# Ten modulation steps of the first FFN: from TensorE row products to weighted sums on VectorE

## What is computed

```python
c_act = silu(c)                                        # 1024 numbers
for l in range(2):
    shift1, scale1, gate1, shift2, scale2, gate2 = split(c_act @ ada_w[l] + ada_b[l], 6)
    if l == 1:
        k_shift, k_scale = split(c_act @ kv_ada_w + kv_ada_b, 2)
    ...
    h = modulate(rms_norm(x, norm2_g[l]), shift2, scale2)
    x = x + gate2 * ((silu(h @ w_gate[l]) * (h @ w_up[l])) @ w_down[l])
```

## Time and profile before

| | |
|---|---|
| median of 3 runs | 1451.62 us (1445.99 to 1454.34) |
| profiled execution: time, span | 1443.54 us, 1441.7 us |
| TensorE busy | 1355.0 us (94%) |
| VectorE busy | 794.1 us (55%) |
| ScalarE busy | 623.7 us (43%) |
| GpSimd busy | 86.3 us (6%) |
| granted TensorE clock, mean | 0.959 |

### The profile page before, as it was taken

One profiled execution on the slowest core, in us unless ns is written; L12 is line 12 of the kernel. 1 busy time (PEld: TensorE's weight loads), 2 busy tenths in 40 slices (PEclk: granted clock), 3 DMA queues, 4 the chain that ended last, 5 costly groups with the idle time before them and its releaser, 6 DMA issues.

```text
span 1441.7 us, 27270 instructions
## 1 busy us (share of the span) xinstructions
PE 1355.0 (94%) x11892; PEld 1241.3 (86%) x11892; DVE 794.1 (55%) x1040; ACT 623.7 (43%) x810; POOL 86.3 (6%) x79
## 2 busy tenths in 40 slices
PE   5579789999999989999999999999999999999998
PEld 4467689999996445999999999999998888999997
DVE  5964664343443365656655565644635755766543
ACT  4742354343343544554434544434542443644342
POOL 6522300000000011000000000000000000000000
PEclk8669799999999989999999999999998999999999
DMA  9606468996564247255556555456353434455452
GB/s 254 197 3 221 134 191 288 306 284 219 179 202 161 88 146 234 88 161 190 175 156 189 184 174 173 160 162 203 95 170 118 146 118 148 143 178 183 159 179 93
DMA packets 237798, 246.91 MB, mean 171 GB/s; under 512 B 5544, under 2 KB 233336, under 8 KB 237704
## 3 DMA queue, kind: packets, MB, share of 16 engines
q1 hardware_dynamic: 236968, 243.82, 53.2%
q0 software_dynamic: 480, 1.57, 0.6%
q10 hardware_dynamic: 256, 0.14, 0.0%
HBM read 244.47 MB, written 1.05 MB: 170 GB/s over the span
## 4 chain that ended last, share of the span: by engine, by line
PE 86%; DVE 6%; ACT 4%; DMA 2%; issue 1%; POOL 0%; SPq 0%; DVEq 0%; ACTq 0%
PE PS L1616 85%; DMA RING<-in_ada_w 1%; DVE ARENA L1397 1%; ACT PARTS L602 0%; DMA RING<-in_w_kv_b 0%; PE PS L2163 0%; DMA RING<-in_w_in 0%; DVE ARENA L1225 0%; DVE ARENA L1222 0%; DVE ARENA L1228 0%; DVE ARENA L1265 0%; DVE WL L1030 0%; DVE ARENA L1411 0%; DVE ARENA L1227 0%; DVE ARENA L1226 0%
## 5 line engine op out<-in xcount | busy, mean ns | idle before, releaser
L1616 PE MATMUL PS<-PARTS 128*128 128x256 f32 (+3 forms) x3652 | 850.4, 284 | 0.0
L1616 PEld LDWEIGHTS PS<-PARTS 128*128 128x128 f32 (+1 forms) x3652 | 627.6, 190 | 1.8 <-issue 1.0
L1030 DVE TENSOR_TENSOR WL<-RING,PARTS 128x2048 fp32r<-128x2048 f32 (+2 forms) x189 | 387.5, 2054 | 295.5 <-ACT PARTS L602 294.9
L1616 PE MATMUL PS<-HH,WL 128*128 128x256 f32 (+3 forms) x1832 | 526.2, 287 | 8.8 <-DVE PARTS L1301 4.0
L1616 PE MATMUL PS<-HH,PARTS 128*128 128x256 f32 (+3 forms) x1832 | 523.0, 286 | 0.0
L602 ACT CAST PARTS<-RING 128x2048 fp32r<-128x2048 f32 (+2 forms) x189 | 323.7, 1715 | 303.5 <-DMA RING<-in_w_ffn_out 68.2
L1616 PEld LDWEIGHTS PS<-HH,WL 128*128 128x128 f32 (+1 forms) x1832 | 349.5, 191 | 15.0 <-issue 7.7
L1616 PEld LDWEIGHTS PS<-HH,PARTS 128*128 128x128 f32 (+1 forms) x1832 | 349.0, 191 | 0.4
L1616 PE MATMUL PS<-PARTS,WL 128*128 128x256 f32 (+1 forms) x832 | 236.0, 284 | 0.4 <-DVE PARTS L1517 0.4
L1616 PEld LDWEIGHTS PS<-PARTS,WL 128*128 128x128 f32 x832 | 157.7, 190 | 1.8 <-issue 1.2
L1616 PE MATMUL PS<-ARENA 128*32 128x63 f32 (+5 forms) x720 | 59.5, 269 | 3.1 <-issue 2.6
(11 more groups left out here) (294 smaller groups left out, 1096.4 us busy)
## 6 DMA issues: line engine op xcount, KB each, us to landing
RING<-in_w_ffn_in SPq DMA_DIRECT2D x44, 1024.0 KB, 5.1
RING<-in_ada_w SPq DMA_DIRECT2D x36, 1024.0 KB, 6.9
RING<-in_ffn_w_gate SPq DMA_DIRECT2D x22, 1024.0 KB, 5.4
RING<-in_ffn_w_up SPq DMA_DIRECT2D x22, 1024.0 KB, 5.4
RING<-in_w_in SPq DMA_DIRECT2D x20, 1024.0 KB, 5.2
ARENA<-in_ada_w SPq DMA_DIRECT2D x12, 1024.0 KB, 8.5
RING<-in_ffn_w_down SPq DMA_DIRECT2D x16, 768.0 KB, 4.4
RING<-in_w_ffn_out SPq DMA_DIRECT2D x16, 768.0 KB, 4.4
```

Source lines behind the costliest of these rows:

```text
L1030: V.tensor_tensor(WL[:, u % SLOTS, 0:w], RING[:, u % SLOTS, 0:w], WH[:, u % SLOTS, 0:w].bitcast(fp32), SUB)\
L1616: return nc.tensor.matmul(o, lhsT, rhs, start=start, stop=stop)
```

## The change

The rows on TensorE, the row copies and MODR are gone for the ten steps. A step becomes two half steps: 1 MB of ADW each (four of the eight k tiles, all 512 columns), which VectorE multiplies by `c_act` and sums into ROWS with four chained instructions (`ada_sum`). Half step n is done by VectorE in pair n for n = 0 to 10, ahead of its wait for silu; halves 11 to 16 stand between the `w_low` of the down projection, two to a chunk; 17, 18 and 19 stand ahead of VectorE's wait for the last chunk. TensorE keeps `ada_cols` (with a column of ones): steps 0 to 4 between the gate and the up unit of pairs 2, 4, 6, 8, 10; steps 5, 6, 7 ahead of chunks 1, 2, 3; steps 8 and 9 behind the down projection and ahead of `stat`. SyncE loads half n into ADW after half n-2 has been summed. VectorE's modulation for the key/value pair and layer 1 moves behind the last additions to X.

```diff
             def ada_load(n):
-                s = ADA_FFN0[n]
+                s, h = ADA_FFN0[n // 2], n % 2
...
-                if n >= 1:
-                    sp.wait_ge(S["ada_rows"], n)
-                for h in range(2):
-                    sp.dma_start(ADW[:, h, :]..., w[:, :, at * 512 + h * 256:at * 512 + (h + 1) * 256])
+                if n >= 2:
+                    sp.wait_ge(S["ada_sum"], n - 1)
+                sp.dma_start(ADW[:, 4 * h:4 * h + 4, :], w[:, 4 * h:4 * h + 4, at * 512:(at + 1) * 512])
...
                     for j in range(MT):
                         if j + 2 < MT:
                             pair(j + 2, j + 2, None)
-                        if j + 1 < len(ADA_FFN0):
-                            ada_load(j + 1)
+                        if j + 2 <= MT - 1:
+                            ada_load(j + 2)
...
+                if kts == "ffn0":
+                    for d in range(16):
+                        take(u + d, ...)
+                        if d in (0, 1, 6, 7, 10, 11, 13, 14, 15):
+                            ada_load(MT + (0, 1, 6, 7, 10, 11, 13, 14, 15).index(d))
...
+            def ada_sum(n):
+                s, h = n // 2, n % 2
+                acc = ROWS[:, s % 2, :]
+                dve.wait_ge(ada_loaded[h], 16 * (s + 1))
+                if h == 0 and s >= 2:
+                    dve.wait_ge(S["ada_cols"], ADA_FRONT + s - 1)
+                if h == 1:
+                    dve.wait_ge(S["ada_sum"], n)
+                for k in range(4 * h, 4 * h + 4):
+                    if k == 0:
+                        ins = V.tensor_scalar(acc, ADW[:, k, :], CACT[:, k:k + 1], None, MUL)
+                    else:
+                        ins = V.scalar_tensor_tensor(acc, ADW[:, k, :], CACT[:, k:k + 1], acc, MUL, ADD)
+                    if k % 4 < 3:
+                        link(ins)
+                ins.then_inc(S["ada_sum"], 1)
...
                     if f == 0:
+                        ada_sum(j)
                         dve.wait_ge(S["silu_ready"], j + (base + 1))
...
                             for d in range(4 * c + 4, 4 * c + 7):
                                 w_low(u0 + d)
+                                if f == 0 and d < 4 * c + 6:
+                                    ada_sum(MT - 2 * c - 4 + d)
+                        elif f == 0:
+                            for n in (17, 18, 19):
+                                ada_sum(n)
...
-                    step = ADA_FRONT + q - 1 if f == 0 and q >= 1 else None
-                    if step is not None:
-                        ada_rows(step)
-                        if q >= 2:
-                            ada_cols(step - 1)
                     for side in range(2):
                         split(u, i)
+                        if f == 0 and side == 1 and q >= 2 and q % 2 == 0:
+                            ada_cols(ADA_FRONT + q // 2 - 1)
...
+                if f == 0:
+                    for c in range(4):
+                        if c >= 2:
+                            pe.wait_ge(S["res_ready"], KT * R_FFN0 + 2 * c - 2)
+                        if c >= 1:
+                            ada_cols(ADA_FRONT + 4 + c)
+                        for h in range(4):
+                            down(c, None, h)
+                    ada_cols(ADA_FRONT + 8)
+                    ada_cols(ADA_FRONT + 9)
+                    return
```

More of the change, by code:

```diff
@@ L451, in _ @@
                 u += 2 * MT
+                if kts == "ffn0":
+                    for d in range(16):
+                        k0, k1 = DOWN_K[d % 4], DOWN_K[d % 4 + 1]
+                        take(u + d, slot(u + d, k1 - k0, 256), down[:, k0:k1, d // 4, :])
+                        if d in (0, 1, 6, 7, 10, 11, 13, 14, 15):
+                            ada_load(MT + (0, 1, 6, 7, 10, 11, 13, 14, 15).index(d))
+                    u += 16
+                    continue
                 with sp.Fori(0, 2) as i:
@@ L687, in row_copy @@
             def row_copy(s):
[L689 to L692, removed]
+                act.wait_ge(S["unit_done"], ada_unit(s) + 2)
                 if s >= 2:
                     act.wait_ge(S["ada_cols"], s - 1)
[L695 to L704, removed]
+                nc.scalar.copy(ROWS[:, s % 2, :], PS[:, 4 if s < ADA_FRONT else 7, :]).then_inc(S["row_copied"], 1)
             def c_compact():
@@ L1321, in _ @@
             ffn(0)
-            dve.wait_ge(S["mod_raw"], 1)
-            for c0, c1, at in ((40, 48, 0), (96, 112, 8), (48, 64, 24)):
-                modulation(c0, c1, MODR[:, at:at + c1 - c0])
+            dve.wait_ge(S["ada_cols"], ADA_FRONT + 5)
+            modulation(40, 48, PS[:, 2, SEQ:SEQ + 8])
+            down_used(0, ADA_GATE2)
+            dve.wait_ge(S["ada_cols"], ADA_LAST)
+            for c0, c1, at in ((96, 112, 8), (48, 64, 24)):
+                modulation(c0, c1, PS[:, 2, SEQ + at:SEQ + at + c1 - c0])
             gain(2, 48 + ADA_SCALE1, VAT["norm1_g"] + KT)
             link(gain(4, KV_SCALE, VAT["kv_norm_g"]))
-            down_used(0, ADA_GATE2)
             rstd(2)
@@ L1673, in ada_rows @@
             def ada_rows(s):
-                n = s - ADA_FRONT
-                ring = s < ADA_FRONT or s >= ADA_LAST
                 if s >= 1:
-                    pe.wait_ge(S["row_copied"], s if ring else s - 1)
+                    pe.wait_ge(S["row_copied"], s if s < ADA_FRONT else s - len(ADA_FFN0))
                 for h in range(2):
[L1680 to L1687, removed]
+                    u = ada_unit(s) + h
+                    loaded(u)
+                    w = slot(u, KT, 256)
+                    b, c0 = 4 if s < ADA_FRONT else 7, h * 256
                     for k in range(KT):
@@ L1690, in ada_rows @@
                         ins = mm(PS[g, b, c0:c0 + 256], CACT[:, k:k + 1].broadcast_to([P, 32]), w[:, k, :], k < 4, k >= 4)
[L1691 to L1694, removed]
+                    ins.then_inc(S["unit_done"], 1)
             def ada_cols(s):
@@ L1705, in ada_cols @@
                     b, at = 2, 384 + 4 * (s - ADA_LAST - 2)
-                pe.wait_ge(S["row_copied"], s + 1)
+                from_sums = ADA_FRONT <= s < ADA_LAST
+                if from_sums:
+                    pe.wait_ge(S["ada_sum"], 2 * (s - ADA_FRONT) + 2)
+                else:
+                    pe.wait_ge(S["row_copied"], s + 1 if s < ADA_FRONT else s + 1 - len(ADA_FFN0))
                 if s >= 4:
                     pe.wait_ge(S["ada_used"], 1)
+                pick = one if from_sums else CN[:, C_SEL:C_SEL + 1]
                 for m in range(4):
-                    ins = mm(PS[:, b, at + m:at + m + 1], ROWS[:, s % 2, m * P:(m + 1) * P], CN[:, C_SEL:C_SEL + 1], True, True)
+                    ins = mm(PS[:, b, at + m:at + m + 1], ROWS[:, s % 2, m * P:(m + 1) * P], pick, True, True)
                 ins.then_inc(S["ada_cols"], 1)
```

27 lines of the change are left out of this document (8 added, 19 removed).

## The result

| | before | after |
|---|---|---|
| median in this comparison | 1449.54 us (1445.99 to 1454.34, 7 runs) | 1461.98 us (1453.41 to 1464.28, 7 runs) |
| ratio, 95% interval | | 1.0074 [1.0047, 1.0100] |
| profiled execution: time, span | 1443.54, 1441.7 us | 1454.1, 1451.9 us |
| TensorE, VectorE busy | 1355.0, 794.1 us | 1346.1, 848.8 us |
| granted clock, mean | 0.959 | 0.949 |

The change costs 0.74% by the ratio, 12.4 us between the two medians. TensorE has less to do and the kernel takes longer.

What follows compares the result with a forecast made beforehand. TensorE was taken to bound the kernel, unbroken for 87.4 us around the change. -3.0 at `stat`, +2.5 for the clock and +2.0 for load starts made +1.5 us, on 1451.6 giving 1453, range 1441 to 1463.

Steps and rivals of the forecast that it cites:

- The outcome that was given 0.68: Whole kernel: the time stays within 0.5% of no change; chance 0.68.
- the outcome given 0.18: Whole kernel: slower by over 0.5%; chance 0.18.
- What is removed: First FFN on TensorE: ten steps' rows go and columns get cheaper, 20.6 us less TensorE work.
- A half step: VectorE's four chained sums: 3.1 us, 2.85 where it begins a step; 2.65 without the cost of links.
- In the pairs it is hidden: FFN pairs: VectorE's 9.1 us of work fits a period of 11.8, so TensorE doesn't stall.
- The ring: Down projection: sum, load, weight load behind it, parts and next sum wait in turn, giving back 17.4 of 20.6 us.
- The ring's size: Down projection: turns from sum 9 to sum 19 take 94.3 us together, so sum 19 ends at 419.8.
- Walk it: Down projection: turn-by-turn count from U8 at 312.9 and sum 9 at 325.5 to sum 19 at 419.8.
- The correction of 2 us for six starts: Down projection: a step's first load took 7.6 us, counted 6.6; a third of that 1.0 added per start, +2.
- TensorE's clock: Work from `stat` on: the 7 us pause ahead of it brings half clock, +2.5 us.
- The slower one: Rival, down projection: modulation and weight loads hold each other up, 1.2 us more per start, 1462 with slower sums; chance 0.14.
- sums of 0.870: Part of the slower rival, VectorE's half steps: each sum instruction takes 0.870 us, adding 4 us.

Runs made afterwards that it cites:

- e2: Changed kernel without the loads of half steps 11 to 19, their sums kept over the bytes of halves 9 and 10; 1427.53 us, ratio 0.9861.
- e3: Changed kernel with four half-step buffers instead of two, so that load n waits for sum n-4; 1429.85 us, ratio 0.9882.
- e9: Changed kernel with half 12's load issued behind D4's weights instead of D1's in SyncE's queue; 1451.96 us, ratio 1.0031.
- e5_own_queue: Changed kernel with the loads of half steps 11 to 19 issued from GpSimd's queue, two buffers kept; 1444.58 us, ratio 0.9963.
- e1: Changed kernel without the loads and sums of half steps 11 to 19, columns on TensorE kept; 1426.05 us, ratio 0.9849.
- e4: Changed kernel with 58 unused matmuls on TensorE ahead of the last partition sums; 1456.63 us, ratio 1.0050.
- e8: Changed kernel with four half-step buffers, and loads and sums of the down projection placed earlier; 1426.27 us, ratio 0.9850.

## Why the prediction was right, and where it was short

The time forecast was 1453.0 in 1441 to 1463; it is 1461.98 by the median, 1 us inside the upper end. In the profiled execution +1.5 us were forecast, and it is +10.6. The mechanism is the one forecast; its size is not. The outcome that was given 0.68, within 0.5% of no change, isn't what came: 0.74% slower belongs to the outcome given 0.18 (the interval begins at 0.47%). And it took some luck to stay in the range: it was set around a median of 1451.6 for the kernel before, of which 1463 is 11.4 us away, while the two medians now lie 12.4 apart.

- **What is removed: right.** U8 was forecast to be done at 312.9 (its own terms give 313.1) and is at 313.27, in an execution that began the FFN 0.4 us later. Without the late halves the gain is 20.8 us, where the forecast had 20.4.
- **A half step: right.** Forecast 3.1 and 2.85, measured 3.10 and 2.8 (0.48, then 2.33), instructions 0.78 us apart. The Trainium skill ("VectorE: DVE Perf Modes", The DRAIN you can't avoid) has eight copies that took as long with a semaphore after each as with one at the end. Carried over to sums that wait for each other, as the forecast did, that makes 2.65, an estimate; the rows after have 3.10. No run here took the links away, so what they cost isn't shown.
- **In the pairs it is hidden: right.** 117.86 us for the ten periods (11.35 and 12.2 give 117.75), and TensorE is unbroken up to 345.01, past the pairs' end.
- **The ring: right as a mechanism.** D2 is issued at 341.4, behind sum 10's end at 340.96; load 19 only behind sum 17. The longest pauses are at D2 and ahead of the last columns (forecast about 4 and 7 us, measured 7.4 and 7.1), and ahead of chunks 2 and 3 TensorE waits for sums 13 and 15 (forecast 2 us each, measured 3.0 and 1.0). e2, e3 and e9 show it from three sides: no loads to wait for, other buffers, another place in the queue. The Trainium skill ("DMA: Bandwidth & Descriptors", Queues, rings and completion order) has each DMA engine take a queue's descriptors in ring order; the rows after agree, D1 lands 3.5 us behind half 11 (326.68 + 8.22 for 331.4).
- **The ring's size: too small. This is the term that failed**, the landing times in "Walk it". Turn by turn, forecast against measured: sum 9 to 10 13.6 and 14.7, to 11 17.6 and 19.0, to 12 4.6 and 4.4, to 13 13.8 and 16.1, to 14 4.6 and 4.4, to 15 13.8 and 15.8, to 17 17.9 and 18.6, to 19 8.4 and 8.4. Together 94.3 and 101.4, and sum 19 ends at 427.7 where the forecast had 419.8; of those 7.9 us it had allowed for 2. 0.7 lie ahead of sum 9 (the FFN's later start, and 5.7 us for U10's landing instead of 5.3), 7.1 in the turns. Three things make most of these. A weight load behind a half adds 3.4 to 3.5 us at D1 and D2, not 2.2 and 1.9. Half 14, issued at 364.42, landed after 7.3 us instead of 5.3; half 13 (issued at 360.00, landed 6.0 later) and D7 (361.45, 6.6) were still under way, where the count let it find an empty queue. And D12 was issued 3.9 us behind half 16, since its slot was only free when TensorE, late itself and at half clock, had used it (380.58 + 8.26 = 388.86 in the chain): the ring also runs through TensorE, which the walk left out. The correction of 2 us for six starts came from the right row, 7.6 us against 6.6, but a third of it was taken where all of it (6 us) and more was due.
- **TensorE's clock: right in kind.** Forecast was 7.0 us from sum 19 to STD with 2.5 for the clock; it is 8.1, with 3.4 for it, because the columns ran at half clock as well as `stat`. The pauses at D2 and at chunk 2 brought half clock too; the forecast said that the ring sets the end there, and at chunk 2 this is what was wrong.
- **The rivals.** The slower one (1462: loads hold each other up, 1.2 us per start) is what the run came to in size, and its half on the loads is right: 7.1 us over six starts are 1.2 each. Its other half, sums of 0.870, was wrong: they take 0.75 (743 to 755 ns). That its total fits so well is in part luck: the clock and what lies behind STD stand in the place of its 4 us for the sums.

So the forecast +1.5 became +8.4 at STD (435.76 for 427.38) by 5.9 from the later end of sum 19 and 1.1 from the clock (8.5, but for rounding), and +10.2 at the span's end by 1.8 us behind STD, which are not settled.

## What to carry to other kernels

Work that is moved to an engine with slack costs what its buffers and its queue cost, not what its instructions cost: here nine half steps of some 3 us cost 1.1 us, and having two buffers instead of four for them cost 24. When a load that waits for an engine is put into an in-order queue, list all loads behind it, follow the ring once around (load, split, sum, next load, and the slots that the slowed engine itself frees), and price each load in the company that it will have, not alone. Then try more buffers and a later place in the queue first; both are small edits.

## What the runs showed of the hardware

- A 768 KB load issued 0.41 us behind a 1 MB load into an empty queue lands 3.5 us behind it (8.22 us after its issue), and a 640 KB load 3.4 us behind (8.16), although such loads took 4.4 and 4.1 by the median before. By bytes it would be 2.2 and 1.9, an estimate from the 3.0 us by which the second of two 1 MB loads landed behind the first.
- In the changed kernel the clock fell to 1.2 GHz in each of the three longest pauses of TensorE, before TensorE had started again: at 349.34 in the one from 345.01 to 352.42, at 380.06 in 377.58 to 380.58, at 424.44 in 420.64 to 427.70. It stayed there for 6.8, 6.8 and 10.2 us.
- Behind shorter pauses it went either way, and their length doesn't tell which. The pause of 1.6 us ahead of 368.13 in e3_four_slots was followed by 3.4 us at half clock, and so was the one of 2.0 us ahead of 397.60 in e5_own_queue; the one of 2.0 us in the changed kernel (414.30 to 416.31) by none. The one ahead of the key/value projection, idle for 2.2 us in each, was followed by 3.4 us in the changed kernel and in e2, and by none in e1, e3, e4 and e8.
- With the late halves in GpSimd's queue, loads of the two queues held each other up: half 19, issued 0.1 us behind a 1 MB weight load of SyncE's queue, took 8.25 us for 5.21, and D8's weights, issued 0.8 us behind half 14, landed 8.2 us after their issue.
